# A five-layer float32 network on one core: waits, order of the products and places of twenty-four modulation blocks changed together

## Time and profile before

| | |
|---|---|
| three runs | 2158.42, 2161.49, 2161.50 us |
| median | 2161.49 us |
| the profiled execution | 2158.44 us, its span 2156.6 us |
| mean granted TensorE clock | 0.988 of full |
| TensorE busy | 2072.9 us, 96% of the span |
| VectorE busy | 1156.1 us, 54% |
| ScalarE busy | 387.4 us, 18% |
| DMA | 292.69 MB, 136 GB/s mean |
| chain that ended last | 86% TensorE, 8% VectorE, 3% DMA |

### The profile page before, as it was taken

How to read it: one execution, slowest core, us unless ns; L and a number is a source line. 1 busy time by engine, 2 the same in 40 slices (tenths; PEclk the granted TensorE clock), 3 DMA queues, 4 the chain that set the end, 5 groups by cost and what they waited for, 6 DMA issues and landing times.

```text
span 2156.6 us, 25033 instructions
## 1 busy us (share of the span) xinstructions
PE 2072.9 (96%) x10918; PEld 1472.8 (68%) x10918; DVE 1156.1 (54%) x1645; ACT 387.4 (18%) x780; POOL 10.7 (0%) x22
## 2 busy tenths in 40 slices
PE   8999898999999999999999989999999999989998
PEld 6887675796448469744884454988884457549973
DVE  2643666474530536653544583455555765646775
ACT  2413110100031410002112361211110011331110
POOL 0000000000000000000000000000000000000000
PEclk9999999999999999999999999999999999999999
DMA  5334686344444334534222101222224453113432
GB/s 195 118 118 172 244 338 253 136 182 166 168 159 161 117 125 164 195 136 148 91 93 102 40 1 39 79 79 79 78 83 165 190 186 131 69 66 130 171 146 114
DMA packets 22749, 292.69 MB, mean 136 GB/s; under 512 B 2752, under 2 KB 3008, under 8 KB 4848
## 3 DMA queue, kind: packets, MB, share of 16 engines
q1 hardware_dynamic: 20864, 280.67, 34.4%
q0 software_dynamic: 1776, 10.43, 1.3%
HBM read 290.03 MB, written 1.05 MB: 135 GB/s over the span
## 4 chain that ended last, share of the span: by engine, by line
PE 86%; DVE 8%; DMA 3%; ACT 1%; issue 0%; SPq 0%; DVEq 0%; ACTq 0%
PE bank L326 85%; DMA ring<-in_W 3%; DVE small L837 1%; PE bank L674 1%; DVE arena L858 1%; DVE arena L636 1%; DVE arena L685 0%; DVE arena L851 0%; PE bank L767 0%; DMA X<-in_x 0%; DVE arena L832 0%; DVE arena L1005 0%; DVE HT L2391 0%; ACT arena L683 0%; DVE arena L1517 0%
## 5 line engine op out<-in xcount | busy, mean ns | idle before, releaser
L326 PE MATMUL bank<-arena 128*128 128x128 f32 (+9 forms) x3856 | 679.1, 351 | 13.5 <-DVE arena L1598 3.7
L326 PEld LDWEIGHTS bank<-arena 128*128 128x128 f32 (+3 forms) x3856 | 475.2, 184 | 201.1 <-issue 157.8
L326 PE MATMUL bank<-HT,ring 128*128 128x128 f32 (+1 forms) x2672 | 461.4, 333 | 13.1 <-DMA ring<-in_W 4.7
L326 PEld LDWEIGHTS bank<-HT,ring 128*128 128x128 f32 x2672 | 410.4, 194 | 59.2 <-issue 21.0
L326 PE MATMUL bank<-ring,arena 128*128 128x512 f32 x690 | 302.9, 594 | 4.0 <-DMA ring<-in_W 4.0
L326 PEld LDWEIGHTS bank<-ring,arena 128*128 128x128 f32 x690 | 130.2, 190 | 165.1 <-issue 164.5
L326 PE MATMUL bank<-ring,HT 128*128 128x512 f32 (+2 forms) x512 | 199.1, 548 | 7.4 <-ACT HT L1950 2.9
L326 PE MATMUL bank<-arena,ring 128*128 128x128 f32 (+2 forms) x1046 | 172.5, 323 | 0.2 <-issue 0.2
L326 PEld LDWEIGHTS bank<-ring,HT 128*128 128x128 f32 x512 | 91.9, 196 | 110.0 <-issue 100.7
L683 ACT ACTIVATE arena<-bank 128x512 f32<-128x512 f32 (+2 forms) x127 | 69.4, 573 | 518.1 <-PE bank L326 487.2
L326 PEld LDWEIGHTS bank<-arena,ring 128*128 128x128 f32 (+1 forms) x1046 | 153.2, 191 | 13.0 <-issue 1.5
(11 more groups left out here) (297 smaller groups left out, 1523.5 us busy)
## 6 DMA issues: line engine op xcount, KB each, us to landing
ring<-in_W SPq DMA_DIRECT2D x125, 2048.0 KB, 7.8
ring<-in_W SPq DMA_DIRECT2D x6, 1536.0 KB, 9.4
ring<-in_W SPq DMA_DIRECT2D x4, 1024.0 KB, 9.6
arena<-in_rel POOLq DMA_DIRECT2D x1, 2048.0 KB, 10.0
arena<-in_rpb POOLq DMA_DIRECT2D x1, 2048.0 KB, 9.3
arena<-in_dft POOLq DMA_DIRECT2D x2, 640.0 KB, 6.6
X<-in_x SPq DMA_DIRECT2D x2, 512.0 KB, 5.9
X<-in_ctx POOLq DMA_DIRECT2D x1, 1024.0 KB, 5.1
```

The source lines that it names most:

```text
L326: return nc.tensor.matmul(out_, lhsT, rhs, start=start, stop=stop, skip_group_check=True)
```

## The change

Nothing is computed differently, apart from zero products at the start whose result nobody reads. In words:

1. `weight_plan` and the three `*_mix` functions: the order of the blocks becomes bqkv0, ada0, ada1, bqkv1, bqkv2, bgate, bab, ada2 to ada23. bqkv0's first half stands ahead of the turns of the inverse, ada0 and ada1 ahead of the rwkv rounds, ada2 to ada4 in and behind rounds 4 and 5; the gdn rounds hold one ada each (11 to 15) and 16 follows them; chunks of gdn hold 17, then two each (18 to 23). Some take the bank of an earlier ada. `pe_mod(1)` moves into `pe_eout`. `dve_y_out` is split, the reciprocal of round 4 moves behind the additions.
2. `seven_order`: (1,1) no longer stands third; chunk 0 is done as a whole first.
3. `pe_seven_rows`: w0 and w1 are taken when a product first needs them.
4. Fronts of `dve_mlp`, `dve_attn` and `dve_ffn(1)`: the second half of tile 1 is added after tile 0's turned data is written (in `dve_ffn(1)` after tile 0 is scaled, its second half after tile 0 is written).
5. `pe_mlp`: the turns of the token tiles stand between the two tiles of the `pproj` product instead of behind them.
6. `act_even`, `dve_even`: ScalarE writes half of the turned tiles, two of the four token sums suffice for "win tokens"; the value tile `vn.0` is copied ahead of the gate rows and of the squares.
7. Start: TensorE runs 12 products on zeros as soon as VectorE has cleared them, and 3 between the two first tiles; SyncE waits for x1 before it issues the large constants and all weight blocks after the first.

```diff
-    for i in range(3):
-        plan += [(f"bqkv{i}", 4096), ada[i]]
-    plan += [("bab", 64), ("bgate", 4096)] + ada[3:]
+    plan += [("bqkv0", 4096)] + ada[0:2] + [("bqkv1", 4096), ("bqkv2", 4096), ("bgate", 4096), ("bab", 64)] + ada[2:]
...
-            seq = [(0, 1), (0, 2), (1, 1), (0, 3), (0, 5), (0, 7), (0, 6), (0, 4)]
+            seq = [(0, j) for j in (1, 2, 3, 5, 7, 6, 4)]
...
-            w0, w1 = (weight(x).rearrange("p (k c) -> p k c", k=KT) for x in names)
+            ws = {}
+            def block(i):
+                if i not in ws:
+                    ws[i] = weight(names[i]).rearrange("p (k c) -> p k c", k=KT)
+                return ws[i]
...
+                w = block(0 if j in (1, 2) else 1) if j in (1, 2, 4) or j == 7 and S[q][2] is None else None
...
+        def pe_fill(n, s, b=None):
+            b = state["bank"] % 8 if b is None else b
+            ps = open_bank("fill", b)
+            for _ in range(n):
+                mm(ps[:, 0:P], s, s, True, True)
+            state["last"][b] = None
...
+            pe_half_block("bqkv0", "bq", 0, 0)
             pe_inverse_first("rwkv", 4, XT1)
             pe_scores("mrb", AV, R)
+            pe_ada(0)
             pe_scores("mrk", KF, R)
...
+            pe_ada(1)
             for k in range(1, 6):
                 for g in range(4):
                     pe_lx("rwkv", k, g, MASKED1, XI1)
                 if k < 4:
-                    pe_half_block(f"bqkv{k - 1}", "bq", 0, 4 * (k - 1))
+                    pe_half_block(f"bqkv{k - 1}", "bq", 1, 4 * (k - 1))
                 elif k == 4:
+                    pe_bgate(1)
                     pe_bab()
-                    pe_bgate(0)
-                    pe_bgate(1)
-                pe_ada(k - 1)
-                if k == 4:
                     pe_bnorm_sum()
-                elif k == 5:
+                else:
+                    pe_ada(3)
                     pe_bnorm_spread()
                 for g in range(4):
                     pe_xlx("rwkv", k, g, LX1, XT1)
-                if k < 4:
-                    pe_half_block(f"bqkv{k - 1}", "bq", 1, 4 * (k - 1))
-            pe_ada(5)
+                if k < 3:
+                    pe_half_block(f"bqkv{k}", "bq", 0, 4 * k)
+                elif k == 3:
+                    pe_bgate(0)
+                elif k == 4:
+                    pe_ada(2)
+            pe_ada(4, banks["rwkv 5.0 XLXt"])
...
+            pe_ada(5)
             pe_ada(6)
-            pe_ada(7)
             pe_chunk_out(0)
+            pe_ada(7, banks["ada5"])
+            pe_chunk_in(1)
             pe_ada(8)
-            pe_chunk_in(1)
+            pe_chunk_out(1)
             pe_ada(9)
-            pe_chunk_out(1)
             pe_ada(10)
...
-                pe_ada(9 + 2 * k)
+                pe_ada(10 + k)
                 for g in range(2):
                     pe_xlx("gdn", k, g, LX2, XT2)
                 if k == 1:
                     pe_mod(0)
-                pe_ada(10 + 2 * k)
+            pe_ada(16)
             pe.wait_ge(vector_done, at("gdn ready"))
...
             for c in range(4):
                 if c > 0:
+                    pe_ada(16 + 2 * c)
                     pe_bchunk_in(c)
-                    pe_ada(20 + c)
+                pe_ada(17 + 2 * c)
                 pe_bchunk_out(c)
-            pe_mod(1)
...
         def pe_start():
+            pe.wait_ge(vector_done, at("fill zero"))
+            pe_fill(12, ADR[:, 0:P])
             pe.wait_ge(loaded["ident"], at("ident in"))
             for t in range(2):
                 pe_turn_tile("mix0", t, XN1)
+                if t == 0:
+                    pe_fill(3, ADR[:, 0:P])
...
+                if t == 0:
+                    for s in range(2):
+                        pe.wait_ge(vector_done, at(f"xt{i} src{s}"))
+                        for h in range(2):
+                            pe_turn(f"xt{i} turned {s}.{h}", [X[:, s, (4 * h + j) * P:(4 * h + j + 1) * P] for j in range(4)])
             pe.mark(f"slot of pproj{i}")
...
-            ready(1)
+            ready(1, (0,))
             dve_turned(f"ffn{i}", 0, gains)
+            ready(1, (1,))
             dve_unit(f"ffn{i}", 1, four(XF[:, 1, :]))
...
+            copy_out(act, "vn.0", VN[:, 0, :])
             act_gate(0, 0, 0)
             act.wait_ge(vector_done, at("win 1 joined1"))
-            squares("qn", QN)
-            squares("kn", KN)
-            for t in range(4):
+            for t in range(1, 4):
                 copy_out(act, f"vn.{t}", VN[:, t, :])
+                if t < 3:
+                    squares(*(("qn", QN), ("kn", KN))[t - 1])
...
                 if i == 0:
+                    sp.wait_ge(loaded["x1"], at("x1 in"))
                     first("const", KC[:, head:], T["const"][:, head:])
```

More of the change, by code:

```diff
@@ L1448, in act_mix @@
                 if k == 4:
-                    ps = full(act, "ab")
-                    p3 = ps[:, 0:16].rearrange("p (t c) -> p t c", t=2)
-                    activation(b3(BETA), p3[:, :, 0:4], ACT.Sigmoid).then_inc(scalar_done, act.one())
-                    activation(b3(ZZ), p3[:, :, 4:8], ACT.Copy).then_inc(scalar_done, act.one())
-                    act.mark("read ab", "ab out")
                     for t in range(2):
@@ L1460, in act_mix @@
                     act.mark("v silu")
+                    ps = full(act, "ab")
+                    p3 = ps[:, 0:16].rearrange("p (t c) -> p t c", t=2)
+                    activation(b3(BETA), p3[:, :, 0:4], ACT.Sigmoid).then_inc(scalar_done, act.one())
+                    activation(b3(ZZ), p3[:, :, 4:8], ACT.Copy).then_inc(scalar_done, act.one())
+                    act.mark("read ab", "ab out")
                     ps = full(act, "bqk ss")
@@ L1711, in dve_mix @@
                         dve_masked("rwkv", k + 1, g, MASKED1, LT1)
+                if k == 4:
+                    dve.wait_ge(scalar_done, at("bqk root"))
+                    nc.vector.reciprocal(INVG, INVG).then_inc(vector_done, dve.one())
+                    dve.mark("bqk inv")
+                    dve_ada(2)
             for c in range(4):
@@ L1786, in dve_mix @@
                         dve_masked("gdn", k + 1, g, MASKED2, LT2)
-                dve_ada(10 + 2 * k)
+                if k == 5:
+                    dve.mark("gdn ready")
                 if k == 1:
@@ L1801, in dve_mix @@
                     dve_y_var()
-            dve.mark("gdn ready")
             for t in range(2):
@@ L1931, in dve_start @@
         def dve_start():
+            nc.vector.memset(ADR[:, 0:P], 0.0).then_inc(vector_done, dve.one())
+            dve.mark("fill zero")
             nc.vector.memset(SCW, 0.0).then_inc(vector_done, dve.one())
@@ L1946, in act_eout @@
             for h in range(2):
+                if h == 1:
+                    act.wait_ge(vector_done, at("ob sq"))
+                    activation(INV2, INV2, ACT.Sqrt, bias=K("eps"), scale=1.0 / P).then_inc(scalar_done, act.one())
+                    act.mark("ob root")
                 for t in range(2):
@@ L1961, in pe_eout @@
                     pe_turn(f"ymix turned {t}.{h}", [Y[:, t, i * P:(i + 1) * P] for i in range(4)])
+                if h == 0:
+                    pe_mod(1)
                 for t in range(2):
@@ L2088, in dve_mlp, with ready @@
             mixed = "aout" if i else "eout"
-            def ready(t):
-                for h in range(2):
+            def ready(t, halves=(0, 1)):
+                for h in halves:
                     dve_add(mixed, h, [t])
@@ L2150, in dve_mlp, with dve_embed @@
             dve.wait_ge(vector_done, dve.n)
-        def dve_embed(i, t):
-            for h in range(2):
+        def dve_embed(i, t, halves=(0, 1)):
+            for h in halves:
                 dve.wait_ge(scalar_done, at(f"sg{i}.{h}.{t}"))
@@ L2485, in dve_ffn, with half @@
             mixed = "oout" if i else "wout"
+            def half(t):
+                dve_add(mixed, 0, [t], gate_row(0))
             def ready(t):
-                for h in range(i == 0, 2):
-                    dve_add(mixed, h, [t], gate_row(0))
+                dve_add(mixed, 1, [t], gate_row(0))
                 dve.wait_ge(vector_done, dve.n)
@@ L2498, in turned @@
                 dve_turned(f"cffn{i}", t, mod_scale(i, 1), mod_shift(i, 1), parts=(0,))
-            for n in ("x0", "u0", "x1", "u1", "t0", "x2", "u2", "t1", "x3", "u3", "t2", "t3") if S == 2 else ("x0", "u0", "x1", "t0", "u1", "t1"):
-                {"x": ready, "u": unit, "t": turned}[n[0]](int(n[1]))
+            for n in ("x0", "u0", "x1", "u1", "t0", "x2", "u2", "t1", "x3", "u3", "t2", "t3") if S == 2 else ("h0", "x0", "u0", "h1", "t0", "x1", "u1", "t1"):
+                {"h": half, "x": ready, "u": unit, "t": turned}[n[0]](int(n[1]))
             nc.vector.memset(F["GV"], 0.0).then_inc(vector_done, dve.one())
@@ L2765, in act_even @@
             act_seven_copy("win 0", 1, 1, EWM1[1])
+            x_turned(0)
+            x_turned(1)
             first(0, 0)
```

86 lines of the change are left out of this document (46 added, 40 removed).

## The result

| | before | after |
|---|---|---|
| four runs each on one chip | 2158.42, 2158.83, 2161.49, 2161.50 us | 2123.13, 2123.55, 2125.40, 2126.54 us |
| median | 2160.16 us | 2124.48 us |
| profiled execution, its span | 2158.44, 2156.6 us | 2126.54, 2124.7 us |

The change makes the kernel faster: ratio 0.9836, 95% interval 0.9819 to 0.9853, 35.7 us by the medians. The two profiled executions lie 31.9 us apart, since before's was its fastest and after's its slowest. The forecast was 2120.0 us, in a range of 2106 to 2136. The total was near; three of its terms, the start, the recurrent layer and the order of the seven products, were not.

The account below looks back on a forecast made before the run. TensorE was busy 2072.9 of 2156.6 us, so only 83.7 us idle and low-clock losses could be won. Terms -20.5 - 13.6 - 14.1 + 10.5 - 1.0 = -38.7 took 2158.4 to 2119.7, stated as 2120.0 us, range 2106 to 2136.

Parts of the forecast that it names:

- the start: Kernel's first tiles and block: x1 landing sooner gains 1.0 us (0 to 1.9); zero products taken as 0 (0 to 4).
- the recurrent layer: 86 to 364 us: moved weight blocks remove waits and low clock, gain 20.5 us, bounds 10 to 26.
- the order of the seven products: down and cdown products: (1,1) no longer covers VectorE's left sums, a loss of 10.5 us, from 7 to 16.
- gain 20.5 us (pool less rest): Recurrent layer: pool of 30.8 us (23.0 idle, 7.8 low clock) less 10.3 us of waits expected to stay.
- the last rival, The fifth: Start: the zero products raise the clock, start gains 4 to 5 us, total 2115 us; chance 0.10.
- a sign of being wrong: Start: the forecast is wrong if the kernel's first block takes 7 instead of 10 us.
- two of three at 1.7: cdown0.0, cdown0.1, cdown1.0: low clock follows two of the three new gaps, 1.7 us each, 3.4 us in the sum.
- Fronts, pproj, even: Two terms: 13.6 us from waits at layer fronts; 14.1 us from pproj turns, even's start and the earlier `vn.0` copy.
- The second: Recurrent layer: waits turn into others at weight queue or VectorE, half the gain goes, 2130 or 2135 us; chance 0.22.
- The third: gdn chunks: ring served one block at a time, 7.8 us per 2 MB block, total 2164 us; chance 0.03.
- the fourth: Seven products: their sums cost nothing because VectorE reaches left 0 sooner, total 2111 us; chance 0.05.

Follow-up runs that it names:

- e7_both: Changed kernel with bonus and bab products 64 columns wide and the old order of the seven products except at down0: 2106.95 us, ratio 0.9761.
- f10_order_only: Kernel before the change with only the new order of the seven products: 2173.93 us, ratio 1.0069.
- e6_wide64: Changed kernel with bonus and bab products writing 64 columns instead of 2 and 8: 2119.13 us, ratio 0.9814.
- f12_fill_more: e7_both with 16, 5 and 4 zero products at the start instead of 12, 3 and 0: 2103.00 us, ratio 0.9743.
- e2_no_fill: Changed kernel without the zero products at the start: 2126.48 us, ratio 0.9841.
- e1_old_order: Changed kernel with the old order of the seven products, (1,1) third again: 2114.93 us, ratio 0.9791.

## Why the prediction was right or wrong

**Right in its total, by two misses of opposite sign.** Against the profiled execution the sum was 6.8 us too good: 9.5 too much for the recurrent layer, 3.3 too little loss for the seven products and 0.8 for small shifts, less 3.0, 1.4 and 2.4 that start, fronts and even gave beyond the forecast. That these nearly cancel is luck; against the medians the forecast was 4.5 us too fast.

**The step that failed** is the last one of the recurrent layer's: "gain 20.5 us (pool less rest)". The pool held 7.8 us of low clock and the rest held none, as if every low clock came from a gap and went with it. The idle part was sized fairly: 10.3 us forecast, 13.4 us in the rows of after (from 20.8 to 366.4 us). More were ada10's 2.13, bqkv1's 1.82 instead of 0.7 and 2.7 instead of 1.5 in the gdn chunks; less the gdn rounds, 2.8 instead of 4.3. The low clock was not: against the version whose clock is 1.00 all through (e7_both, 322.7 us busy from first block to output product) the same stretch cost before 10.8 us more (333.5) and after 9.5 (332.2). The forecast took back 7.8; 1.3 came. The pool itself was too small: by the earlier trace rows the low clock takes up to 3.5 us from the window of 248 (0.14 x 25), of which 1.7 were counted, and up to 1.7 from that of 273 (0.03 x 56.3), of which none was.

What the runs showed in its place: the clock falls behind the narrow bonus and, less surely, behind bab, and it stays up when they are written 64 columns wide. At the gate block the forecast's trace had both, 3.64 us of narrow bab rows and a gap of 1.64, and the forecast took the gap alone. At the bonus it gave no sign, as this was before's timeline there:

```profile
90.79 3.84 PE L326 MATMUL bank<-arena 64*128 64x128 f32 x64 [0.63 <-DVE arena L1517]
94.57 1.95 PE L326 MATMUL bank<-KC,arena 128*128 128x2 f32 x16
96.37 3.76 PE L326 MATMUL bank<-arena 128*128 128x64 f32 x32
```

lv is at full clock here, and the window from 96 to 112 us has 1.00. But this was one execution of two: f10_order_only has the same rows in the same old layer, and 0.79. As far as two profiles tell, before's had escaped by chance, and why the changed layer meets the low clock in six of six is not shown; it even has a wide row more, ada0 at 94.14, between the turns and the bonus. In e6_wide64, e7_both and f12_fill_more the layer gains 19.6, 19.0 and 20.5 us, near the forecast's 20.5, but made up otherwise: in e7_both 10.8 of clock and 8.2 of idle time, where the forecast had 7.8 and 12.7.

**The start** was sized at 1.0 us for x1 and nothing for the zero products. In the profile it gave 4.0 us, as in the last rival, and a sign of being wrong came true: the first block took 7.17 us, not 10. The reason given for taking 0, that the turns had not raised the clock either, did not hold for the zero products. But that was half luck: the block runs at full clock in four of nine profiles with zero products and in none of five without, mean 8.5 against 9.5 us; the second turn took 1.1 to 1.5 us with them and 1.97 without. In the medians the zero products are worth 2.0 us, not told from nothing, and neither is the 1.0 us for x1. The rule on transposes that the prediction cites from the Trainium skill ("TensorE: Matmul & The Clock Gate", section "Part 4: PE-mode transpose") is not tried by these runs: zero products and turns were never exchanged for one another.

**The seven products.** Gaps forecast 2.8, 3.7 and 4.0, measured 2.93, 3.74 and 4.07: the working, from when VectorE gets to the sums, holds. The term missed by 3.3 us because the clock fell behind all three and for longer at the first. By profile this loss varies: cdown0.0's first rows behind the gap took 3.67 us in e2_no_fill and 6.63 in after, for the same 8 instructions. It is a chance, and "two of three at 1.7" put it too low: the clock cost 6.5 us beside the gaps here, not 3.4.

**Fronts, pproj, even.** Each step came as worked out. mlp0 gave 6.0 us where the forecast says 5.3, but its own terms add up to 5.7 (3.72 less 0.7, 6.52 less 3.8). `vn.0` gave 7.8 instead of 6.2 us mostly because the low clock behind its gap (1143 to 1151 us) cost 3.4 us, not "some 2".

**Rivals.** The second had the layer's size, about half the gain (11.0 of 20.5 us), but mostly not its mechanism: the ring costs 2.13 us where the DMA share is 1.00, the gdn chunks wait 2.7 us in all for blocks, and the gdn rounds wait less than forecast. Of the 9.5 us missed 6.5 are clock and 3.0 idle time. The third falls: at 364 GB/s in the chunks a 2 MB block comes every 5.8 us, not 7.8, and no gap there is over 1 us. No cdown gap is missing, so the fourth falls. The fifth, the zero products, came in the changed kernel's profile and in three of the eight others that have them.

## What to carry to other kernels

Read the low clock by its own rows and ask what TensorE did ahead of it, gap or not: behind products of a few columns it fell here as behind a wait, and writing 64 columns instead of 2 cost nothing (2.00 against 1.95 us for 16 instructions). A product that needs only a weight block is worth its place ahead of one that waits for sums: here it was worth 9.6 to 14.8 us over the five products. A profile's low clock differs from execution to execution, so a term of it is a chance and wants several profiles or a median.

## What the runs showed of the hardware

- Behind 16 instructions of 2 columns TensorE's clock went from 2.4 to 1.2 GHz while the engine was busy: window 98 to 112 us, busy for 14.00 of 14.00, clock 0.63; the last gap before the row, 0.91 us, ends 4.9 us ahead of it. The clock was low there in all six profiles of the changed layer that have this row behind `mrk`. With 64 columns, at the same 0.12 us per instruction, it stayed at 1.00 in three of three of that layer and in one of the old.
- The same instructions meet the low clock in one execution and not in another: the first block took 7.17, 8.86, 9.61, 9.67 and 10.12 us in kernels whose start is the same. The Trainium skill, "TensorE: Matmul & The Clock Gate", section "Part 1: The HAM clock gate (the "warmup" mystery)", says that the count of slow products of one kernel varies from run to run; the traces, one of each such kernel, agree.
- Ahead of the first fall the clock column can't be relied on: in the profiles without zero products it shows 1.00 from 16 to 18 us, where the window counts 6 or 7 instructions of 128x256; in the changed kernel's profile, at the full clock, it counts 11. In e1_old_order, with zero products and a block of 9.67 us, the column does show the low clock from 12 to 19 us.
